# The last eight rows of a modulation vector moved from behind the routing into the w_o stage

## The reference

```python
mod = c_act @ w_ada[l] + b_ada[l]
sh1, sc1, g1, sh2, sc2, g2 = [m[:, None, :] for m in jnp.split(mod, 6, axis=-1)]
h = rmsnorm(x, norm1_g[l]) * (1 + sc1) + sh1
qkv = h @ w_qkv[l]
...
y = jnp.concatenate([rmsnorm(y_a, swa_out_g[l]), rmsnorm(y_b, moba_out_g[l])], axis=-1) @ w_o[l]
x = x + g1 * y
h = rmsnorm(x, norm2_g[l]) * (1 + sc2) + sh2
x = x + g2 * hier_moe(h, w_group[l], b_group[l], w_expert_router[l], b_expert_router[l],
                      w_gate[l], w_up[l], w_down[l])
return rmsnorm(x, final_g)
```

## Time and profile before

| what | us |
|---|---|
| median of 3 runs | 1431.66 |
| lowest and highest | 1430.23, 1432.35 |
| the profiled execution | 1430.98 |
| its span (first to last instruction) | 1429.1 |

### The profile page before, as it was taken

How to read it: one execution, slowest core, us unless ns; L and a number is a source line. 1 busy time by engine, 2 the same in 40 slices (tenths; PEclk the granted TensorE clock), 3 DMA queues, 4 the chain that set the end, 5 groups by cost and what they waited for, 6 DMA issues and landing times.

```text
span 1429.1 us, 14957 instructions
## 1 busy us (share of the span) xinstructions
PE 1311.6 (92%) x5797; PEld 663.2 (46%) x5797; DVE 681.7 (48%) x1069; ACT 158.0 (11%) x424; POOL 62.1 (4%) x74
## 2 busy tenths in 40 slices
PE   4999999999999999999997998989899799888896
PEld 4686688577888635333332332333233233223332
DVE  5678788699987621432332331333233232232235
ACT  3300000295001302000000000000000000000002
POOL 1000000013000100000000000000000000000000
PEclk9999999999999999999999999999999999999999
DMA  9999999983999999999999999999999999999995
GB/s 337 394 396 387 399 401 392 392 287 117 397 400 422 354 426 425 425 425 423 427 427 427 425 425 427 423 430 425 425 427 427 427 425 425 428 425 428 423 425 206
DMA packets 102961, 569.11 MB, mean 398 GB/s; under 512 B 5216, under 2 KB 19808, under 8 KB 70272
## 3 DMA queue, kind: packets, MB, share of 16 engines
q1 hardware_dynamic: 102384, 567.67, 97.5%
q0 software_dynamic: 528, 0.78, 0.4%
HBM read 566.27 MB, written 2.16 MB: 398 GB/s over the span
## 4 chain that ended last, share of the span: by engine, by line
PE 68%; DMA 26%; DVE 2%; ACT 2%; issue 1%; SPq 1%; DVEq 0%; ACTq 0%
DMA ring<-in_w_up 25%; PE PS L1731 22%; PE PS L1490 12%; PE PS L1695 8%; PE PS L1784 6%; PE PS L1596 6%; PE PS L1493 4%; PE PS L1568 2%; DMA ring<-in_w_ada 1%; PE PS L1678 1%; PE PS L1657 1%; PE PS L1716 1%; PE PS L1517 1%; PE PS L1431 0%; PE PS L1746 0%
## 5 line engine op out<-in xcount | busy, mean ns | idle before, releaser
L1731 PE MATMUL PS<-ring,gysq 128*64 128x512 f32 x960 | 222.7, 619 | 40.6 <-DMA ring<-in_w_up 40.6
L1731 PE MATMUL PS<-ring,W 128*64 128x512 f32 x1024 | 236.7, 620 | 21.4 <-DMA ring<-in_w_up 21.4
L939 DVE SCALAR_TENSOR_TENSOR W<-ring,sm,W 128x1024 f32<-128x1024 f32 (+1 forms) x195 | 234.4, 1202 | 21.7 <-DMA ring<-in_w_ada 5.7
L1784 PE MATMUL PS<-ring,W 128*64 128x512 f32 x992 | 219.7, 595 | 12.4 <-ACT W L864 12.4
L1267 DVE TENSOR_TENSOR r<-r,PS 128x512 f32<-128x512 f32 x120 | 82.5, 687 | 232.2 <-PE PS L1695 232.2
L1490 PE MATMUL PS<-r,ring 128*128 128x256 f32 x768 | 167.2, 379 | 0.7 <-DVE r L978 0.7
L1731 PEld LDWEIGHTS PS<-ring,gysq 128*64 128x64 f32 x960 | 79.3, 143 | 183.2 <-issue 183.2
L1490 PEld LDWEIGHTS PS<-r,ring 128*128 128x128 f32 x768 | 145.7, 190 | 22.9 <-issue 3.4
L1731 PEld LDWEIGHTS PS<-ring,W 128*64 128x64 f32 x1024 | 76.6, 142 | 170.2 <-issue 170.2
L1272 DVE TENSOR_SCALAR W<-W 128x256 f32<-128x256 f32 x32 | 21.0, 658 | 280.4 <-ACT W L860 279.6
L1784 PEld LDWEIGHTS PS<-ring,W 128*64 128x64 f32 x992 | 69.4, 137 | 142.3 <-issue 134.4
(11 more groups left out here) (273 smaller groups left out, 833.7 us busy)
## 6 DMA issues: line engine op xcount, KB each, us to landing
ring<-in_w_gate SPq DMA_DIRECT2D x64, 2048.0 KB, 25.5
ring<-in_w_up SPq DMA_DIRECT2D x64, 2048.0 KB, 28.0
ring<-in_w_down SPq DMA_DIRECT2D x64, 2048.0 KB, 28.4
ring<-in_w_ada SPq DMA_DIRECT2D x32, 2048.0 KB, 18.1
ring<-in_w_ada SPq DMA_DIRECT2D x32, 1024.0 KB, 16.2
ring<-in_w_qkv SPq DMA_DIRECT2D x9, 2048.0 KB, 19.0
ring<-in_w_o SPq DMA_DIRECT2D x8, 2048.0 KB, 17.6
ring<-in_w_qkv SPq DMA_DIRECT2D x8, 1536.0 KB, 16.9
```

What stands on the lines that cost most here:

```text
L939: ins = V.scalar_tensor_tensor(total, w, cT[:, t:t + 1], total, ALU.mult, ALU.add)
L1731: last = mm(PS[64 * j:64 * j + 64, i % 2, :].rearrange("p (m n) -> p m n", m=2), hE[i % 2][:, k], w[:, :, t, 256 * j:256 * j + 256], start ...
L1784: last = mm(PS[64 * q:64 * q + 64, bank + i2, :], hidT[:, b, 64 * j:64 * j + 64], w[:, b, 512 * ch:512 * ch + 512], start=(j + b == 0), st ...
```

## The change

`stream_plan` puts chunks (12, 2) and (12, 3) straight behind (12, 0) and (12, 1), so they lie in slots 2 and 3, and the experts' first chunk goes to slot 4 and not to slot 2. All expert chunks come behind them in one run. `WO_ROWS` grows from 56 rows to 64, and the eight rows behind the routing are gone. No row, byte or matmul is added or dropped.

```diff
@@ -218,9 +218,8 @@
             wo(g + 1, 0)
         if g == 0:
             order.append(("more", 1, None, None, None))
+    rows(LAST, 2, 3)
     first = sum(o[2] is not None for o in order) % RING
-    for k in (2, 3):
-        order.append(("rows", (LAST, k), (first + 4 + k) % RING, "rows", ROW_NO[LAST, 4 * k + 3]))
@@ -449,7 +448,7 @@
-        WO_ROWS = [[2, 2, 2, 2], [12, 2, 1, 1], [12, 2, 1, 1], [14, 1, 1, 0]]
+        WO_ROWS = [[2, 2, 2, 2], [13, 2, 2, 1], [13, 2, 2, 1], [15, 1, 1, 3]]
@@ -538,9 +537,6 @@
-                if (kind, i) == ("rows", (LAST, 2)):
-                    for m in range(6):
-                        expert_load(m)
@@ -593,7 +589,7 @@
-            for m in range(6, EXP_CHUNKS * E):
+            for m in range(EXP_CHUNKS * E):
                 expert_load(m)
@@ -1305,8 +1301,6 @@
-            for _ in range(8):
-                row()
```

## The result

| | median us | runs |
|---|---|---|
| before | 1430.95 | 6, 1428.41 to 1434.96 |
| after | 1438.72 | 6, 1438.24 to 1440.26 |

The change makes the kernel slower, by a ratio of 1.0056 with a 95% interval of 1.0041 to 1.0070, that is by 7.8 us. The forecast was 1436.5 in a range of 1432.5 to 1440.0: the right side and inside the range, but a growth of 4.8 us where 7.8 came. The profiled execution of the changed kernel took 1439.37 us, its span 1437.5.

A forecast was written before the change was run, and what follows sets the result against it. The stream of weights was taken to set the end. Chunk 8's issue, 493.5 + 5.4 (VectorE) + 0.4 (clock) = 499.3, plus 8.5 lands at 507.8 against 503.0: +4.8 on 1431.66 gives 1436.5 us, range 1432.5 to 1440.0.

The forecast's parts named there:

- part 1: Expert loads, chunks 0 to 8: without delay the reordered stream lands chunk 8 at 502.0, 1.0 us sooner.
- The hole at 480: DMA dip at 480 to 487 us in the kernel before, 197 GB/s, 3.8 us lost; forecast to be gone.
- The restart: Chunk 8 issued to DMA engines that have run dry: 8.5 us from issue to landing, as seen on chunk 6.
- rival B: Rows late as forecast, but chunk 8 lands 5 to 7 us after issue: 1432.8 to 1435 us, chance 0.15.
- part 2: VectorE in the w_o stage: eight more rows add 11.0 us, some 5.6 in gaps; residual(15) 5.4 us late.
- part 3: TensorE at the routing's start: over 4 us idle lowers its clock, costing 0.4 us, between 0 and 1.6.
- the one number to forecast: Chunk 8's landing, said to move the end with it: 507.8 against 503.0 us, +4.8 us.
- sixth sign: Expected in the changed kernel's profile: no DMA hole from the one at 493 to 500 us to the end.
- rival C: Residual(15) late as forecast and chunk 8 landing 8.5 us after issue: 1434.8 to 1438.5 us, chance 0.62.
- rival D: Later still, first_gate_up moving 8 us or more, or TensorE idle beyond 6 us at 460: 1438.5 to 1442, chance 0.10.
- second wait: In the experts' first group, where chunk 10 and on are issued by TensorE's progress; adds to an end 7 us or more late.
- middle stretch: Measured time within 1428.8 to 1434.5 us, between the faster and slower outcomes: chance 0.19.

The follow-up runs named there:

- experiment 4: Changed kernel's load order, but rows 201 to 208 left behind the routing as before the change: median 1430.59 us, ratio 0.9994 to the kernel before.
- experiment 2: Changed kernel with rows 201 to 208 cut to 8 of 1024 columns, otherwise the row table of before: 1430.65 us, ratio 1.0000 to the kernel before.
- experiment 3: Changed kernel with the row table of before in its second and third group, all added rows in the last: 1439.33 us, ratio 1.0060 to before.
- experiment 1: Changed kernel with seven spare 256-column matmuls on TensorE ahead of router_part(15): median 1435.63 us, ratio 1.0036 to the kernel before.
- experiment 7: Kernel before, with six spare additions (about 4.3 us) on VectorE ahead of the eight rows behind the routing: 1433.0 us, ratio 1.0012.

## Why the prediction was right, and where it was too small

**Order of the loads (part 1): right.** The hole at 480 closed, the stream ran dry again ahead of chunk 8, and experiment 4 shows the order alone at nothing. The restart was put at 8.5 us from issue to landing; it took 7.7, and 7.6 in experiment 2, which is above rival B's 5 to 7 as well, and the 0.8 us did not reach the end. The fixed cost that the prediction took from the Trainium skill, DMA: Bandwidth & Descriptors, section "Anatomy of one DMA", is given there for transfers issued through GpSimd. These are SP's, and 7.7 less the 4.9 of a full stream is 2.8, not 2.0. The hole ahead of chunk 8 was put at 493 to 500 and stood from about 490 to 502.

**Rows in the w_o stage (part 2): right, within 0.3 us.** The wait for chunk (11, 2) was worked out from 418.6 to 422.6 and is 4.25 us long; residual(12) 4.9 us late, measured 5.1 (452.20 + 0.94 - 448.00); residual(15) 5.4 us late, measured 5.3. The sentence that "the data set the pace" needs what experiment 3 added: the work sets the same pace.

**TensorE's clock (part 3): the mechanism right, the term mis-sized.** The prediction took 0.4 us with an upper bound of 1.6, and 2.7 came (2.5 by experiment 1). This is the larger part of the 3.0 us by which the forecast growth was too small. The bound was read off one fall, in which the clock was back after some 3.4 us; here it stays at 0.50 for about twice as long (464.5 to 471.3, from the granted clock of the windows), and the routing's start, taken for a mix of short matmuls and waits, turned out to be TensorE's nearly throughout: it is busy 7.4 of 8 us there (464 to 472) in experiment 1, at full clock. By the Trainium skill, TensorE: Matmul & The Clock Gate, section "Why this matters for your kernels", idle gaps between bursts of matmuls bring the clock back to half and should be avoided; the trace agrees (3.47 us of idle, then 0.50), and experiment 1 shows the remedy.

**What sets the end: the step that failed.** The prediction made the landing of chunk 8 "the one number to forecast" and said of TensorE's further delay that "1 us of that doesn't matter". It does. The reason given was that "chunk 8 and each later one is issued well before its predecessor lands". Chunk 26 of the kernel before is issued at 584.05, 3.5 us before chunk 25 lands (569.78 + 17.8 = 587.6); in the changed kernel it is 2.5 us (591.14, and 576.87 + 16.7 = 593.6), in experiment 2 2.2 us, and in these two the DMA engines ran short there. TensorE was not ahead of the stream's need but level with it: the chunks up to the middle of the second group of four experts (chunk 41, at 643 us) are issued by TensorE's progress, with so little to spare that a chunk 8 that is 2.0 us early (experiment 2) is worth nothing, and that in the changed kernel a further 1.3 us were lost behind it (the window at 590 to 600; the prediction's own sixth sign, a hole behind 505, as "a cost that I left out"). The landing of chunk 8 moved by +5.3 us on the span's clock (500.6 + 7.7 against 493.5 + 9.5), the stream at 670 by +6.6. With TensorE's delay, 5.8 us as predicted, in place of the stream's 4.8, the forecast would have been 1437.5; with the clock's real price as well, 1439.8, a growth of 8.1 us against the measured 7.8 (the measured time of before is 0.7 below the 1431.66 that the sum starts from).

**The rivals and the range.** The measured 1438.72 lies just above rival C's 1438.5, the likeliest, and inside rival D's 1438.5 to 1442. D had named the second wait, at chance 0.10. Of its two points, 8 us at first_gate_up was reached, and idle time of TensorE beyond 6 us was not (3.47). The range held the time because it reached beyond C's bounds, not because the sum had the right terms. The chance of 0.19 for the middle stretch is a little below what its own parts add up to, about 0.21.

## What to carry to other kernels

A hole in a transfer that bounds the kernel is worth something only if what issues the next transfers is not level with it: look for the next wait that the stream meets, and at how many microseconds it has to spare there. Before work is moved into gaps of an engine, lay the landings of its data beside the gaps; a gap ahead of data that hasn't landed is no room. Where a moved step makes TensorE wait in front of a chain of short matmuls, price the fall of its clock over the whole chain, or give it spare matmuls in the wait.

## What the runs showed of the hardware beyond the expectation

After 3.47 us without work TensorE's granted clock stayed at half, 1.2 GHz, for some 6.8 us, and after 5.81 us of wait in experiment 3, with its start in the wait itself, until about 473 us. One and the same gap can go either way: behind 2.25 us of idle time in the last group the granted clock was 0.87 in the profile before and 1.00 in experiment 7's. Seven spare calls, 3.29 us of matmuls, kept it at 1.00 in the wait and delayed nothing (the matmul behind them still waited 0.25 us for residual(15)). A 2 MB load issued to idle DMA engines landed 7.2 to 8.5 us after its issue, while in a full stream one landed every 4.9 us.
